# Two orders at once: mLSTM outputs by token with denominators in a column, and the first softmax half ahead of a slot's first evacuation

## What is computed

```python
# sliding-window attention, per head, blocks of 128 queries on 256 keys
m = maximum(max(scores), sink);  p = exp(scores - m)
probs = p / (sum(p) + exp(sink - m));  out = probs @ v

# mLSTM, per head and direction: log_d = cum_t - cum_s + ig_s, lower triangular
m_t = max(log_d, axis=-1);  scores = (q @ k.T) * exp(log_d - m_t)
num = scores @ v;  den = sum(scores, axis=-1)
h = num / maximum(abs(den), exp(-m_t))
# forward + backward, then head_rmsnorm(h) * g * sigmoid(m_o)
```

## Time and profile before

| | us |
|---|---|
| median of 3 timed runs | 2348.64 |
| timed runs, lowest to highest | 2343.47 to 2349.5 |
| profiled execution | 2342.4 |
| its span, first to last instruction | 2340.6 |
| mean granted clock of PE | 0.980 |

### The profile page before, as it was taken

The page is one execution under the profiler, slowest core; times in us unless marked ns, Lnnn a source line. Parts: engine busy times, 40 slices in busy tenths (PEclk is TensorE's granted clock), DMA queues, the critical chain, the costliest instruction groups (busy, mean ns, idle before and its releaser), DMA issues.

```text
span 2340.6 us, 26933 instructions
## 1 busy us (share of the span) xinstructions
PE 2216.8 (95%) x10044; PEld 1780.8 (76%) x10044; DVE 1270.9 (54%) x1970; ACT 820.8 (35%) x1194; POOL 101.2 (4%) x79
## 2 busy tenths in 40 slices
PE   6999999999999999999999999998786999999998
PEld 6888888777666778778888878887554867888886
DVE  7886776764555443443333376656565454443443
ACT  4522222232323442242222254444453334332332
POOL 3000000100000000100000030000000101000001
PEclk9999999999999999999999999999897999999999
DMA  7654554422212223223323222112111312333332
GB/s 287 233 189 148 178 188 152 167 77 72 73 54 63 81 73 99 87 76 99 99 90 99 88 93 64 55 55 81 54 54 34 119 45 81 100 99 93 104 91 72
DMA packets 65108, 237.83 MB, mean 102 GB/s; under 512 B 7328, under 2 KB 7456, under 8 KB 64240
## 3 DMA queue, kind: packets, MB, share of 16 engines
q1 hardware_dynamic: 61344, 220.90, 29.0%
q0 software_dynamic: 2512, 13.47, 1.8%
q10 hardware_dynamic: 1152, 2.10, 0.2%
HBM read 232.21 MB, written 4.23 MB: 101 GB/s over the span
## 4 chain that ended last, share of the span: by engine, by line
PE 81%; DVE 11%; ACT 5%; issue 2%; DMA 1%; SPq 0%; DVEq 0%; ACTq 0%
PE bank L1777 22%; PE bank L1778 22%; PE bank L1779 22%; PE bank L2075 2%; PE bank L1814 2%; DVE work L1061 2%; PE bank L1816 2%; PE bank L1815 2%; PE bank L1952 1%; DVE wlo L1052 1%; PE bank L1977 1%; ACT work L694 1%; ACT whi L531 1%; DVE work L1227 1%; PE bank L2151 1%
## 5 line engine op out<-in xcount | busy, mean ns | idle before, releaser
L1777 PE MATMUL bank<-hhi,whi 128*128 128x512 f32 x1536 | 613.6, 399 | 5.8 <-DVE hlo L1098 3.1
L1052 DVE TENSOR_TENSOR wlo<-raw,whi 128x1024 fp32r<-128x1024 f32 (+1 forms) x353 | 430.7, 1220 | 324.5 <-ACT whi L531 322.1
L1779 PE MATMUL bank<-hhi,wlo 128*128 128x512 f32 x1536 | 601.1, 391 | 0.0
L1778 PE MATMUL bank<-hlo,whi 128*128 128x512 f32 x1536 | 601.1, 391 | 0.0
L531 ACT ACTIVATE whi<-raw 128x1024 fp32r<-128x1024 f32 (+1 forms) x353 | 368.0, 1043 | 475.7 <-PE bank L1779 411.2
L1777 PE MATMUL bank<-ghi,whi 128*128 128x512 f32 (+1 forms) x976 | 372.9, 382 | 18.2 <-DVE wlo L1052 14.7
L1778 PE MATMUL bank<-glo,whi 128*128 128x512 f32 (+1 forms) x976 | 368.8, 378 | 0.0
L1779 PE MATMUL bank<-ghi,wlo 128*128 128x512 f32 (+1 forms) x976 | 368.7, 378 | 0.0
L1777 PEld LDWEIGHTS bank<-hhi,whi 128*128 128x128 f32 x1536 | 290.2, 189 | 79.0 <-issue 12.6
L1779 PEld LDWEIGHTS bank<-hhi,wlo 128*128 128x128 f32 x1536 | 289.7, 189 | 61.6
L1778 PEld LDWEIGHTS bank<-hlo,whi 128*128 128x128 f32 x1536 | 290.2, 189 | 60.6 <-issue 2.9
(11 more groups left out here) (264 smaller groups left out, 2017.7 us busy)
## 6 DMA issues: line engine op xcount, KB each, us to landing
raw<-w SPq DMA_DIRECT2D x393, 512.0 KB, 3.6
work<-w SPq DMA_DIRECT2D x16, 512.0 KB, 7.2
raw<-w SPq DMA_DIRECT2D x16, 384.0 KB, 3.1
work<-rows_hbm POOLq DMA_DIRECT2D x8, 512.0 KB, 5.9
xT<-x_t POOLq DMA_DIRECT2D x1, 2048.0 KB, 10.8
kv_hbm<-work POOLq DMA_DIRECT2D x2, 1024.0 KB, 4.4
work<-kv_hbm POOLq DMA_DIRECT2D x2, 1024.0 KB, 6.0
y_t<-xT ACTq DMA_DIRECT2D x8, 256.0 KB, 2.2
```

The lines of the kernel that those rows point to most:

```text
L1052: nc.vector.tensor_tensor(wlo[v % 2][:, 0:kc * P], raw[u % 4][:, 0:kc * P], whi[v % 2][:, 0:kc * P].bitcast(F32), ALU.subtract).then_inc(w ...
L1777: nc.tensor.matmul(dst, wh[:, ws], hi[:, c, :], start=c == 0, stop=False)
L1778: nc.tensor.matmul(dst, wh[:, ws], lo[:, c, :], start=False, stop=False)
L1779: ins = nc.tensor.matmul(dst, wl[:, ws], hi[:, c, :], start=False, stop=c == kc - 1)
```

## The change

Attention: on both engines, the weight split, `softmax_first(i)` and `step_exp(i)` come ahead of `conv_unit` or `gate_unit` of the slot's first unit; `step_turned` and `take_output` stay behind it.

mLSTM:

- The values get a 129th column of ones (`ml[..]["v"]` is now 4 × 129). `values_over(h, b)` takes each 128×128 block of `sT` as stationary operand and the 129 columns as moving one: five matmuls per source block, whose results are token-major, 128 tokens in the partitions, with the denominator in column 129. `token_out` gives their place: banks 6, 7 forward, 5, 3 backward.
- `denominators(h)` (DVE) copies the eight columns out, takes the maximum of den, −den and exp(−m), and the reciprocal, on 128×8. exp(−m) comes from `floor_col`: eight small matmuls turn the row −t−cum to columns after `acol`'s, and ACT takes one Exp. The rows' Exp, two stores and the `em` DMAs are gone.
- `forward(h)` (ACT) writes the four forward blocks, scaled by the reciprocal, to `tok`; `both(h)` (DVE) adds the backward ones, block by block.
- `token_norm(h)` (ACT): four squares with sums to a column, Ln and Exp on 4 columns, four scaled copies. `turn_back(h)` (PE): four transposes to bank 4. `ml_out` (DVE) is now one instruction.
- `magnitudes`, `steps`, and `head_sum` and `head_rstd` for the mLSTM heads are gone.
- The orders of all three engines are written anew from U+5 to the first two units of `V_WO2`. On PE, unit U+15 is cut into parts between the blocks of head 3, where before parts of `V_WO2` stood. On ACT, `decays` of heads 2 and 3 is cut in two by other steps.

```diff
-                    for lhs, dst in ((v, bank[6 + dr]), (ones, bank[(5, 3)[dr]])):
-                        if dr == 1 and b > 0:
-                            nc.tensor.matmul(dst[:, 0:b * P], lhs, sT[h % 2][:, at_:at_ + b * P], start=False, stop=False)
-                        own = b * P - t0 if dr == 1 else 0
-                        ins = nc.tensor.matmul(dst[:, t0 + own:t1], lhs, sT[h % 2][:, at_ + own:at_ + t1 - t0], start=b == 0,
-                                               stop=last)
+                    for j in range(t0 // P, t1 // P):
+                        i, d = 2 * dr + j // 2, at_ + j * P - t0
+                        ins = nc.tensor.matmul(token_out(dr, j, P + 1), sT[h % 2][:, d:d + P], ml[h % 2]["v"][:, b, :],
+                                               start=(b, j) == first[i], stop=(b, j) == final[i])
+            def denominators(h):
+                dve.wait_ge(nd_done, h + 1)
+                for dr in range(2):
+                    for i in range(2):
...
+                        ins = nc.vector.tensor_copy(den_col[:, at_:at_ + 2].unsqueeze(2), den)
+                ins.then_inc(den_step, 1)
...
+                stt(larger, dens, -1.0, view(floor_col[:, h:h + 1], [8 * NB + 4, 2], [8, NB]), ALU.mult,
+                    ALU.max).then_inc(den_step, 1)
...
+                nc.vector.reciprocal(den_col, den_max).then_inc(den_step, 1)
+            def both(h):
+                for j in range(NB):
+                    dve.wait_ge(fwd_done, NB * h + j + 1)
+                    stt(tok[:, j, :], token_out(1, j, P), den_col[:, NB + j:NB + j + 1], tok[:, j, :], ALU.mult,
+                        ALU.add).then_inc(both_done, 1)
+            def forward(h):
+                act.wait_ge(den_step, 4 * h + 4)
+                if h > 0:
+                    act.wait_ge(tok_turned, h)
+                for j in range(NB):
+                    nc.scalar.activation(tok[:, j, :], token_out(0, j, P), ACT.Copy,
+                                         scale=den_col[:, j:j + 1]).then_inc(fwd_done, 1)
+            def token_norm(h):
+                for j in range(NB):
+                    act.wait_ge(both_done, NB * h + j + 1)
+                    ins = nc.scalar.activation(square[0][:, j * P:(j + 1) * P], tok[:, j, :], ACT.Square,
+                                               accum_out=square_col[:, j:j + 1])
...
+            def turn_back(h):
+                pe.wait_ge(tok_done, h + 1)
+                if h < NH2 - 1:
+                    pe.wait_ge(vtok_done, 2 + NH2 + h + 2)
+                else:
+                    pe.wait_ge(op_src, NH2 + h)
...
```

The new order on ACT, and on PE around heads 2 and 3:

```diff
-            decays(0)
             head_rstd(NH2 - 1)
+            decays(0)
...
             silu_qk(1, 1)
-            group_values(U + 6)
             decays(1)
             after_unit(U + 7)
-            magnitudes(0)
+            group_values(U + 6)
+            forward(0)
+            token_norm(0)
             after_unit(U + 8)
...
+            split_next(U + 12)
+            decays(2, 0, 1)
+            forward(1)
+            decays(2, 1, NB)
+            group_unit(U + 11)
             group_values(U + 10)
+            token_norm(1)
...
+            forward(2)
+            decays(3, 0, 2)
             group_values(U + 14)
+            decays(3, 2, NB)
+            token_norm(2)
...
-            unit(U + 5, H)
+            unit_part(U + 5, H, 0, 4)
             head_sum(NH2 - 1)
+            unit_part(U + 5, H, 4, DC)
...
+            unit_part(U + 15, H, 0, 3)
             pair(3, 0)
+            unit_part(U + 15, H, 3, 5)
             group_turn(U + 14)
-            unit(U + 15, H)
-            num_den(3, 0)
+            values_over(3, 0)
             pair(3, 1)
+            unit_part(U + 15, H, 5, 7)
+            values_over(3, 1)
             pair(3, 2)
+            unit_part(U + 15, H, 7, DC)
+            values_over(3, 2)
+            turn_back(2)
             pair(3, 3)
+            unit_part(V_WO2, G, 0, 3, first=(op_ready, J_Y2))
+            values_over(3, 3)
```

And in the attention loop of DVE (ACT alike, with `step_exp`):

```diff
                 for a, v in enumerate(units):
+                    if a == 0:
+                        split_next(v)
+                        softmax_first(i, prob, lo, True, SCORE_SCALE)
                     if a == 1:
                         split_next(v)
                         softmax_last(i, prob, lo, True)
                     (conv_unit if v < V_CP else lambda u: gate_unit(u, V_CP))(v)
-                    if a == 0:
-                        softmax_first(i, prob, lo, True, SCORE_SCALE)
-                        if i > 1:
-                            take_output(i - 2)
+                    if a == 0 and i > 1:
+                        take_output(i - 2)
```

More of the change, by code:

```diff
@@ L40 @@
 EVENTS = 3 + LEVELS + 1
-ML_STEPS = 7
 MLP_PARTS = 4
@@ L850, in silu_qk, with decays @@
                                      bias=vcol("mconv_b", 4 * k + h)).then_inc(qk_done, 1)
[L852 to L865, removed]
+            def decays(h, first=0, last=NB):
+                if first == 0:
+                    act.wait_ge(dm_done, 2 * h + 2)
+                    if h >= 2:
+                        act.wait_ge(nd_done, h - 1)
+                for b in range(first, last):
                     for dr in range(2):
@@ L1660, in _ @@
+            denominators(0)
+            split_next(U + 8)
+            both(0)
             decayed(1, 0)
+            unit_evac(U + 8)
             decayed(1, 1)
+            split_next(U + 9)
+            taps(2, 0, 2)
+            decayed(1, 2)
+            after_unit(U + 9)
             ml_out(0)
-            after_unit(U + 9)
+            taps(2, 2, 5)
             operand_lo(J_Y2 + NH2, NH2)
-            taps(2, 0, 4)
-            decayed(1, 2)
-            taps(2, 4, 10)
+            decayed(1, 3)
@@ L1668, in _ @@
+            taps(2, 5, 8)
             masked_rows(2)
-            decayed(1, 3)
             after_unit(U + 10)
-            steps(1)
+            taps(2, 8, 10)
+            denominators(1)
+            both(1)
             after_unit(U + 11)
-            after_unit(U + 12)
             decayed(2, 0)
+            unit_evac(U + 12)
             decayed(2, 1)
+            split_next(U + 13)
+            taps(3, 0, 2)
+            after_unit(U + 13)
+            decayed(2, 2)
             ml_out(1)
-            after_unit(U + 13)
@@ L1679, in _ @@
-            operand_lo(J_Y2 + NH2 + 1, NH2 + 1)
-            taps(3, 0, 4)
-            decayed(2, 2)
-            taps(3, 4, 10)
-            masked_rows(3)
-            decayed(2, 3)
-            after_unit(U + 14)
+            taps(3, 2, 5)
+            decayed(2, 3)
+            taps(3, 5, 8)
+            after_unit(U + 14)
+            taps(3, 8, 10)
+            masked_rows(3)
+            denominators(2)
+            both(2)
+            operand_lo(J_Y2 + NH2 + 1, NH2 + 1)
             decayed(3, 0)
-            steps(2)
+            decayed(3, 1)
@@ L1689, in _ @@
+            decayed(3, 2)
             after_unit(U + 15)
-            decayed(3, 1)
             ml_out(2)
+            decayed(3, 3)
             operand_lo(J_Y2 + NH2 + 2, NH2 + 2)
-            decayed(3, 2)
-            decayed(3, 3)
-            steps(3)
+            denominators(3)
+            both(3)
             ml_out(3)
@@ L2050, in _ @@
             ins.then_inc(acol_done, 1)
+            for dr in range(2):
+                for b in range(NB):
+                    at_ = (dr * NB + b) * 8
+                    ins = nc.tensor.matmul(bank[7][:, at_:at_ + 8], row[f"cum{dr}"][0:8, b * P:(b + 1) * P],
+                                           ident[0:8, 0:8], start=True, stop=True)
+            ins.then_inc(floor_in, 1)
             def hg_item(h, z):
@@ L2174, in _ @@
+            group_turn(U + 6)
             unit(U + 8, H)
             pair(1, 0)
-            head_sum(NH2)
             unit_part(U + 9, H, 0, 4)
-            num_den(1, 0)
+            values_over(1, 0)
             pair(1, 1)
             unit_part(U + 9, H, 4, DC)
-            num_den(1, 1)
+            values_over(1, 1)
+            turn_back(0)
             pair(1, 2)
             unit_part(U + 10, H, 0, 4)
-            num_den(1, 2)
+            values_over(1, 2)
             pair(1, 3)
@@ L2187, in _ @@
             unit_part(U + 10, H, 4, DC)
-            num_den(1, 3)
+            values_over(1, 3)
             unit(U + 11, H)
```

196 lines of the change are left out of this document (98 added, 98 removed).

## The result

The changed kernel takes 2261.8 us (2259.6 to 2262.09, 4 runs) against 2348.86: ratio 0.9632, 95% interval 0.9615 to 0.9649. Its profiled execution takes 2261.72, span 2259.9. Forecast were 2274 in a range of 2256 to 2298.

What follows compares the result with a forecast made beforehand. The prediction took TensorE (PE), busy 95% of the span, as the bound. Terms −15.3, −18.7, −29.4, −10 and +1.8 sum to −71.6, from 2342.4 to 2270.8; with half of 6.2 added, 2274, range 2256 to 2298.

Steps and rivals of the forecast that it cites:

- Attention: Attention: eight PE waits for ACT's copy of the turned block vanish (13.6 us), plus 1.7 of slow clock: −15.3 us.
- PE work: mLSTM stage: five 129-column matmuls a block replace `num_den`, four transposes replace each head sum: −18.7 us.
- The rival of unhidden weight loads: mLSTM values: weight loads don't hide behind matmuls, 80 × 0.21 = 17 us, giving 2291; chance 4 in 100.
- Idle time: mLSTM stage: PE's 50.0 us of idle time falls to 20.6, mostly at head boundaries: −29.4 us.
- The walk through the queues: mLSTM stage: new orders of three engine queues, timed with old-trace prices, leave PE 17.6 us of waits.
- The 3.0 added for hand-overs: mLSTM stage: allowance for some 30 hand-overs between engines, each 0.06 to 0.2 us where exposed: 3.0 us idle.
- Clock in the stage: mLSTM stage and just after: 19.5 us lost to slow clock, 9 left for two or three slow stretches: −10 us.
- Floor columns: PE's path at `acol`: eight more matmuls of 8 columns at 0.22 each: +1.8 us.
- The rest: Stretch from the last chunk of head 3 to the end of the kernel: no change, 0 us.
- The level: Whole kernel: half of the 6.2 us by which the profiled execution lay below the timed median, added to 2270.8.
- Against the first: Rival, mLSTM stage: ACT's or DVE's queue takes over, heads 1 to 3 wait longer: 2299 or 2286; chance 18 in 100.
- The clock and hand-overs were kind: Rival: no 3.0 us of hand-over slop and no slow clock stretch, giving 2260; chance 13 in 100.

Runs made afterwards that it cites:

- by doubling: The changed kernel with each of the 80 matmuls of 129 columns issued twice into the same sums: 2275.11 us, ratio 0.9703.
- the floor columns late: The changed kernel with the eight small matmuls that turn the floor rows moved into the first HGRN head: 2261.71 us, ratio 0.9645.
- the four transposes: The changed kernel with the sixteen matmuls of 8 columns for decay and floor rows replaced by four 128x128 transposes: 2256.18 us, ratio 0.9623.

## Why the prediction was right, and where it was off

- **Attention: right, the clock by halves.** −15.3 forecast, −15.4 measured, and 15.3 with this order alone (306.7 to 291.4). The 13.6 of waits all came. Of the clock I took 1.7 of 3.4; the stretch at 654.8 went, 3.4 back, but one of 3.4 us stood in the first unit, 1.7 lost. That one isn't the change's: the second trace of the changed kernel has none there, and its attention takes 289.8. So the agreement to 0.1 is luck.
- **PE work: right.** 1.13 us a block forecast, 1.12 measured; 0.222 a matmul by doubling. The rival of unhidden weight loads is out. In all 19.6 against 18.7.
- **Idle time: right in mechanism, and the term that was mis-sized.** 20.6 us were forecast, the trace has 11.3: 9.3 of the 10.7 us by which the stage beat the forecast. The walk through the queues gave 17.6 us in 12 waits. The places were nearly all right: 0.3, 2.0, 0.9 and 1.2 for head 2 were 0.2, 1.0, 0.4 and 0.7; 2.2 and 4.8 for head 3 were 2.1 and 3.9; the 2.3 of the last operand 2.3. The waits of 0.5, 0.4 and 0.8 didn't come, those of 1.2 and 1.0 in the last head came as 0.4: each was a small difference of two times, and there the walk errs. The 3.0 added for hand-overs were no idle time at all: 115.3 us of stage less 11.3 idle and 1.5 of clock leave 102.5, where the priced work is 99.4 (one head sum lies ahead of the stretch now). The kernel before has the same surplus, 184.5 less 50.0 and 12.0 leave 122.5 against 119.0 priced. It stands on both sides and should have been left out.
- **Clock in the stage: nearly right, from a wrong start, with luck.** I took all that was left of the stage before, 15.5 us, for the clock, and 9 of 19.5 as what stays. By its slow stretches the clock cost 12.0 there; the other 3.5 are the surplus above. In the trace of the changed kernel 1.5 stay. This is the kindest trace: with the same waits or nearly so, its second trace and the three other kernels whose stage is unchanged (the attention's old order, the floor columns late, the four transposes) lose 2.7 to 3.4 in it, and three of these four have one more stretch of 3.4 us behind the last operand. One or two slow stretches in the stage and one behind it is what to expect.
- **Floor columns: mis-sized the other way.** +1.8 forecast, +3.2 measured. The matmuls' own time was right (1.8 us for eight); I hadn't priced the clock behind them, 1.7 for a slow stretch of 6.8 us in place of 3.4.
- **The rest: right** in that nothing moved (−0.9). I had counted 4 us back behind the stage, where the clock is now 1.00; a wait for a weight (1.8, before 1.2) stands there, and a later slow stretch is longer by 3.4.
- **The level.** The time lies 12.2 below the forecast: 10.7 for the stage and 3.1 that I had added because the profiled execution before was a quick one, less 1.6 in the other stretches.
- **Rivals.** None came alone. Against the first I had written that DVE and ACT both lose work; DVE does, but ACT's rose from 81.8 to 85.5 us. The clock and hand-overs were kind, forecast at 2260 with 13 in 100: that is where the time landed, but mostly by the walk's waits and not by the clock, and 57 on 2262 to 2286 was too much.

## What to carry to other kernels

Where PE waits at the boundary of a loop, lay the chain that it waits for beside PE's next work, and walk the orders of all queues with durations from the trace: the places come out right, and each wait within 1 us. Don't add an allowance for hand-overs that the kernel before has too. Price an idle gap with the slow clock behind it, read from the slow stretches and not from what a sum leaves over: here 38.7 of the stage's 68.8 us were waits, 10.5 the clock, and 19.6 the smaller work, most of it the halved matmuls. Trace a kernel twice before a difference of 1 to 2 us is put down to an edit: slow stretches come and go by themselves. Denominators wanted per token come with the values as a 129th column, from a column of ones in the moving operand; they then lie as a few values on each partition, where a reciprocal costs 0.2 us and not 3.4.

## What the runs showed of the hardware

- Groups of matmuls of 8×8 are followed by a granted clock of 0.50 although PE issues without a gap: 3.4 us behind one group, 6.8 behind two, 6.8 behind a second one a unit later; with transposes of 128×128 in their place none. Whether it is their few columns, their few rows or the 1.8 us that a group lasts wasn't tried.
- The length of a wait doesn't settle whether a slow stretch follows. The wait of 3.9 us in the stage brought 3.4 us in one trace and 6.8 in four others, one of them of the same kernel; 4.65 brought 6.8. The 2.3 for the last operand brought 3.4 to 10.2 us in eight of eleven traces and none in three, and of the two traces of the changed kernel one has it. The 2.1 ahead of pair(3, 0) brought one in three of nine. In the kernel before, a wait of 2.4 in the attention was followed by 6.8 us, and others of 2.4 by none.
- A weight load of 128×128 in float32 hid behind a matmul of 129 columns at 0.222 us, all rows in use. With 64 columns such a matmul takes 0.21, with 8 columns 0.23.
